# A ninth weight slot in an encoder layer's mixture of experts: the residual sums move into the rows buffer, and LayerNorm 2's constants are fetched last

## The chip, the cores and the metric

One core of a Trainium2 chip runs the whole program. The metric is the device time of one execution in microseconds; the times of before are three executions. Five engines work side by side and wait for each other by semaphores: PE (TensorE, matrix products), DVE (VectorE), ACT (ScalarE), POOL (GpSimd) and SP (SyncE, which here does nothing but issue transfers). The transfers run on 16 DMA engines.

## The reference, cut to what matters

One layer for 256 prompt frames and 32 sample frames of width 1024: LayerNorm 0, a combined projection, sparse attention and causal pooling, an output projection, LayerNorm 1, then a mixture of experts (top 4 of 32, softmax over the kept logits) and LayerNorm 2. What the change touches is the end:

```
h1 = LN1(2**0.25 * h + mix)                      # 288 rows of 1024
for e in range(32):
    gu   = h1 @ w1[e] + b1[e]                    # w1[e]: 1024 x 2048, f32, 8 MB
    gate = min(gu[:, :1024], 7); up = clip(gu[:, 1024:], -7, 7)
    act  = (up + 1) * gate * sigmoid(1.702 * gate)
    out += gates[:, e] * (act @ w2[e] + b2[e])   # w2[e]: 1024 x 1024, f32, 4 MB
y = LN2(2**0.25 * h1 + out)
```

All 32 experts' weights in f32, 32 x 12 MB (MB of 2^20 bytes here and for slots), are read once, and are nearly all that the program reads.

## The kernel before

**Passes.** Each expert's rows are handled in passes of 64 rows (BLK). With these inputs there are 32 passes, one for an expert, in a runtime loop over pairs: an even pass 2i and an odd pass 2i+1, and a last pair written out after the loop. In a pass (`expert` on PE, L981) the rows gathered before are multiplied by w1 (`up_products`, L891: eight parts k of 128 features; 64 products of L905), DVE and ACT make the clamped SwiGLU (L1629 to L1636, L1267), PE turns the result and multiplies by w2 (`down_products`, L921: two halves, 16 products of L931 each), and the product is added, weighted by the gates, to the sums of all 288 rows (`combine`, L965 on PE; `accumulate`, L1651 on DVE, for three tiles of 128 rows). While it does so it gathers the rows of the next pass (`gather_rows`, L869) from `rows_b`: the normalised rows split once, before the first pass, into three bf16 parts (ACT L1239 and L1242, DVE L1611 and L1614).

**Slots.** A pass needs 12 MB of weights. They come in eight slots of 2 MB (SLOT): `ring` slots 0 and 1 hold the first half of w1 of an even pass, `late` (two slots) that of an odd pass; ring slots 2 and 3 hold the second half of w1 (its third and fourth part) of every pass, and ring slots 4 and 5 the two halves of w2 of every pass. PE frees a slot when its last product has read it (`slot_free`, `odd_free`; slot 3's stands for the end of all up products). So before the loop eight slots are filled: pass 0's six and pass 1's first half.

**Order of the fetches.** SP issues them in an order written out by hand, each behind a wait for its slot; what stands behind a waiting issue waits too. For the first four pairs (WIDE_PAIR = 4, passes 0 to 7 releasing) it is `in_order_of_release` (L494), in narrow fetches of 2 MB: first half of pass 2i+2, rest (slots 2, 3, 4, 5) of 2i+1, first half of 2i+3, rest of 2i+2. Then LayerNorm 2's two constants are fetched (L514, L515; 512 KB each, spread over 128 partitions). Then comes `in_order_of_use` (L502) in wide fetches of 4 MB, each for a pair of slots and behind the release of both: slots 2 and 3 of 2i+1, slots 4 and 5, first half of 2i+2, slots 2 and 3, slots 4 and 5, first half of 2i+3. POOL counts up the second slot's semaphore for a wide fetch. The last pairs are narrow again.

**Buffers.** `rows` holds the layer's rows and, after the split into bf16 parts, nothing more: its tiles 1 and 2 take LayerNorm 2's constants (`ln2`), its tile 0 small things of the last pass. The sums live in `out_acc`, 12 KB per partition of `area`, a buffer that the input projection's and the output projection's weights had before; small scratch of the routing, the expert biases in bf16 (`bias_parts`) and the pooling's running sums are in `area` as well.

**The end.** After the last pass PE adds its two halves to the sums in PSUM (`start_sum`, `add_last`), DVE takes the statistics (L1698), centres with the constants (L1706), ACT and POOL or DVE finish, and three transfers write the result.

Of the kernel before, what the change touches and what calls it, by code (L numbers as in the profile page):

```python
# [22 lines left out]
P = 128  # L23
# [16 lines left out]
def encoder_kernel(nc, ins, outs):  # L40
# [32 lines left out]
    with ExitStack() as ctx:  # L73
# [7 lines left out]
        ring = sb("ring", [P, NSLOT, SLOT])  # L81

        area = sb("area", [P, KT * IN])
# [39 lines left out]
        out_acc = area[:, KT * D:KT * D + NT * D].rearrange("p (t n) -> p t n", t=NT)  # L123
        sums_a = area[:, KT * D:KT * D + 4 * UW].rearrange("p (g n) -> p g n", g=4)
        sums_b = area[:, KT * D + 4 * UW:KT * D + 8 * UW].rearrange("p (g n) -> p g n", g=4)
        BP = KT * D + NT * D

        bias_parts = area[0:3 * NE, BP:BP + 3 * F // 2].bitcast(BF16)
        last_u = area[0:POOL_PAST, BP + 3 * F // 2:BP + 3 * F // 2 + D].rearrange("p (s c) -> p s c", s=2)
        assert BP + 3 * F // 2 + D <= KT * IN  # L130
        flat = area[:, BP + 3 * F // 2:BP + 3 * F // 2 + D]
# [25 lines left out]
        spare = ring[:, 2:6, :].rearrange("p s n -> p (s n)")  # L157
# [21 lines left out]
        probs = carve(spare, 8 * 288)  # L179
        assert used[0] <= 4 * SLOT  # L180
# [4 lines left out]
        pick = carve(area, NT * BLK).bitcast(BF16).rearrange("p (t h s) -> p t h s", t=NT, h=2)  # L185
        g_sb = carve(area, F // 2)
# [10 lines left out]
        last_giveT = rows[:, 0, 0:TOKP]  # L197
        last_y = rows[:, 0, TOKP:TOKP + D // 2]
        ln2 = rows[:, 1:3, :]
# [34 lines left out]
        odd_free = [sem(f"odd_free{s}") for s in range(2)]  # L234
        bias_in = sem("bias_in")
# [119 lines left out]
        w1_t = ring[:, 0:4, :].rearrange("p s (k n) -> p (s k) n", k=2)  # L355
        w1_odd = late[:, :].rearrange("p (k n) -> p k n", k=4)
        w2_t = ring[:, 4:6, :].rearrange("p s (c n) -> p s c n", c=4)
# [42 lines left out]
        def _(sp):  # L400
# [31 lines left out]
            for s in range(2):  # L432
                sp.dma_start(ring[:, s, :], w1_part(0, s)).then_inc(w_in_slot[s], 16)
# [15 lines left out]
            sp.dma_start(ring[:, 2, :], w1_part(0, 2)).then_inc(w_in_slot[2], 16)  # L449
            sp.wait_ge(lastu_sb, 1)  # L450
            sp.dma_start(pool_prompt[0, 0], last_u[:, 0, :]).then_inc(rows_out, 16)
            sp.dma_start(pool_sample[0, 0], last_u[:, 1, :]).then_inc(rows_out, 16)
# [3 lines left out]
            sp.dma_start(ring[:, 3, :], w1_part(0, 3)).then_inc(w_in_slot[3], 16)  # L456
# [3 lines left out]
            for h in range(2):  # L460
                sp.dma_start(ring[:, 4 + h, :], w2_v[0, h]).then_inc(w_in_slot[4 + h], 16)
# [5 lines left out]
            def first_half(i, e, odd, wide):  # L467

                base, ready, free = (late[:, :], w_in_odd, odd_free) if odd else \
                    (ring[:, 0:2, :].rearrange("p s n -> p (s n)"), w_in_slot, slot_free)  # L470
# [10 lines left out]
            def rest(p, e, wide):  # L481

                for s in (2, 4) if wide else (2, 3, 4, 5):
                    if wide:
                        src = w1_v[col(e), 1] if s == 2 else w2_whole[col(e)]
                        dst = ring[:, s:s + 2, :]
                        sp.wait_ge(slot_free[s + 1], p)
                    else:
                        src = w1_part(col(e), s) if s < 4 else w2_v[col(e), s - 4]
                        dst = ring[:, s, :]  # L490
                    sp.wait_ge(slot_free[s], p)
                    sp.dma_start(dst, src.rearrange("e p n -> p (e n)")).then_inc(w_in_slot[s], 16)

            def in_order_of_release(i):  # L494

                even = expert_of(sp, 2 * i + 2)
# [5 lines left out]
            def in_order_of_use(i, wide):  # L502

                rest(2 * i + 1, expert_of(sp, 2 * i + 1), wide)
                even = expert_of(sp, 2 * i + 2)
                first_half(i, even, False, wide)
                rest(2 * i + 2, even, wide)
# [13 lines left out]
            sp.dma_start(y_prompt[0, P:2 * P, :], out_acc[:, 1, :]).then_inc(final_out, 16)  # L521
# [3 lines left out]
        def _(pool):  # L525
# [50 lines left out]
            pool.wait_ge(ln_in[2], 32)  # L576
            with pool.Fori(WIDE_PAIR, last_wide(pool)) as i:
                for first, p in ((w_in_slot, 2 * i + 1), (w_in_odd, 2 * i + 2)):
                    for s in (2, 4):
                        pool.wait_ge(w_in_slot[s], 16 * (p + 1))  # L580
                        pool.sem_inc(w_in_slot[s + 1], 16)
# [4 lines left out]
            nc.gpsimd.tensor_tensor(out_acc[:, 0, :], out_acc[:, 0, :], ln2[:, 1, :], ALU.add).then_inc(result[0], 1)  # L586
# [3 lines left out]
        def _(pe):  # L590
# [300 lines left out]
            def up_products(x, e, i, odd):  # L891
# [5 lines left out]
                for k in range(KT):  # L897
                    if k % 2 == 0 and k < 4:
                        pe.wait_ge((w_in_odd if odd else w_in_slot)[k // 2], 16 * (i + 1))
                    elif k % 2 == 0:  # L900
                        pe.wait_ge(w_in_slot[k // 2], 16 * (e + 1))
                    w = w1_odd[:, k] if odd and k < 4 else w1_t[:, k]
# [4 lines left out]
                    if k % 2 == 1 and k < KT - 1:  # L907
                        last.then_inc((odd_free if odd and k < 4 else slot_free)[k // 2], 1)
# [4 lines left out]
                last.then_inc(slot_free[3], 1)  # L913
# [124 lines left out]
            def start_sum(t, e):  # L1038
# [4 lines left out]
                for g in range(2):  # L1043
                    mm(ps_sum[t][0:n, g, :], ident[0:n, 0:n], out_acc[0:n, t, g * 512:(g + 1) * 512],
# [14 lines left out]
        def _(act):  # L1059
# [151 lines left out]
            copy(last_u[:, :, :], ps[0:POOL_PAST, 4:6, :]).then_inc(lastu_sb, 1)  # L1211
# [28 lines left out]
            for t in range(NT):  # L1240
                act.wait_ge(part_rest, t + 1)
                copy(rows_b[:, t, 1, :], rows[:, t, :]).then_inc(part_mid, 1)  # L1242
# [48 lines left out]
            nc.scalar.activation(out_acc[:, 0, :], out_acc[:, 0, :], ACT.Copy, scale=rstd[:, 0:1]).then_inc(scaled, 1)  # L1291
# [3 lines left out]
            nc.scalar.activation(ps_sum[1], out_acc[:, 1, :].rearrange("p (g n) -> p g n", g=2), ACT.Copy,  # L1295
# [4 lines left out]
            act.dma_start(y_prompt[0, 0:P, :], out_acc[:, 0, :]).then_inc(final_out, 16)  # L1300
            act.wait_ge(result[2], 1)
            act.dma_start(y_sample[0], out_acc[0:TS, 2, :]).then_inc(final_out, 16)
# [4 lines left out]
        def _(dve):  # L1307
# [293 lines left out]
            for t, (_, n, _) in enumerate(tiles):  # L1601
# [3 lines left out]
            v.tensor_scalar(giveT[:, :], out_acc[:, 0, 0:TOKP], 0.0, None, ALU.mult).then_inc(giveT_ready, 1)  # L1605
            v.tensor_scalar(y_sb[:, :], out_acc[:, 0, :], 0.0, None, ALU.mult).then_inc(y_ready, 1)

            dve.wait_ge(x_gathered, 1)
            for t in range(NT):
                dve.wait_ge(part_high, t + 1)  # L1610
                v.tensor_tensor(rows[:, t, :], rows[:, t, :], rows_b[:, t, 0, :], ALU.subtract).then_inc(part_rest, 1)  # L1611
            for t in range(NT):
                dve.wait_ge(part_mid, t + 1)
                v.tensor_tensor(rows_b[:, t, 2, :], rows[:, t, :], rows_b[:, t, 1, :], ALU.subtract).then_inc(split_ready, 1)  # L1614
# [23 lines left out]
            def swiglu_half(q, e):  # L1638

                g_q, u_q = quads(g_sb, q), quads(u_sb, q)  # L1640
                dve.wait_ge(slot_free[3], e + 1)
# [9 lines left out]
            def accumulate(t, comb, want, done, src=ps_c):  # L1651
                _, n, _ = tiles[t]
                dve.wait_ge(comb, want)
                acc = out_acc[0:n, t, :].rearrange("p (h n) -> p h n", h=2)
# [4 lines left out]
            def expert(e, last=False):  # L1659
# [15 lines left out]
                swiglu(slot_free[3], gate_ready, sig_ready, up_ready, prod_ready, e + 1, h_ready)  # L1675
# [27 lines left out]
            def centre(t):  # L1703

                n = tiles[t][1]
                v.scalar_tensor_tensor(halves(out_acc[0:n, t, :]), ps_sum[t][0:n], moments[0:n, t, 0:1],  # L1706
# [10 lines left out]
            v.tensor_tensor(halves(out_acc[:, 1, :]), ps_sum[1], halves(ln2[:, 1, :]), ALU.add).then_inc(result[1], 1)  # L1717
            centre(2)
            row = out_acc[0:TS, 2, :]
# [29 lines left out]
```

## Time and profile before

| | us |
|---|---|
| three executions | 1094.59, 1095.67, 1095.62 |
| their median | 1095.62 |
| the profiled execution | 1094.63 |
| its span, first to last instruction | 1092.8 |

The granted TensorE clock is 0.997 over the span. Busy in the span: PE 1039.7 us, DVE 399.3, ACT 238.2, POOL 15.1. Matmul ends are modelled, so a busy PE is not PE at its peak. "us to landing" of a transfer is counted from its issue on SP to the semaphore that says it has arrived, and so holds its time in the queue. Numbers at the start of a row are us from the span's start.

### The profile page before, as it was taken

The page shows a single profiled execution, that of the slowest core. Times are in us where ns is not written, and L with a number is a line of the kernel's source. Part 1 is how long each engine was busy: PE and PEld are TensorE (multiplying, and loading weights), DVE is VectorE, ACT ScalarE, POOL GpSimd, SP SyncE. Part 2 cuts the span into 40 slices and gives each one's busy share as a digit, 9 for nine tenths or more (in the row PEclk, how much of TensorE's full clock was granted, in tenths as well). Part 3 has the DMA queues.
Part 4 walks back from the last instruction along what each step waited for, and adds up shares of the span by engine and source line. Part 5 has one row for each costly group of instructions (what it writes and reads, how often), then busy time and mean ns, then how long its engine had stood idle before and what let it go on. Part 6 is the DMA issues. An engine that isn't in the chain of part 4 may idle for free.

```text
span 1092.8 us, 13939 instructions
## 1 busy us (share of the span) xinstructions
PE 1039.7 (95%) x5251; PEld 424.5 (39%) x5252; DVE 399.3 (37%) x721; ACT 238.2 (22%) x472; POOL 15.1 (1%) x28
## 2 busy tenths in 40 slices
PE   8989999999999999999999999999999999999996
PEld 7755463333333333333333333333333333333332
DVE  7894275333332233333222233333332322323226
ACT  3334123112222112222211122222211111222112
POOL 1003000000000000000000000000000000000000
PEclk9999999999999999999999999999999999999999
DMA  9750538999999999999999999999999999999991
GB/s 318 293 231 3 231 154 361 426 428 430 427 428 431 428 432 431 428 435 428 435 428 435 429 434 429 434 429 434 429 434 429 434 429 434 431 433 422 427 428 76
DMA packets 28556, 421.81 MB, mean 386 GB/s; under 512 B 5325, under 2 KB 5965, under 8 KB 11546
## 3 DMA queue, kind: packets, MB, share of 16 engines
q1 hardware_dynamic: 28346, 420.93, 91.1%
q10 hardware_dynamic: 192, 0.66, 0.2%
q8 instruction: 10, 0.16, 0.1%
q14 instruction: 8, 0.07, 0.0%
HBM read 420.11 MB, written 1.46 MB: 386 GB/s over the span
## 4 chain that ended last, share of the span: by engine, by line
PE 54%; DMA 34%; DVE 10%; issue 1%; ACT 0%; SPq 0%; DVEq 0%; ACTq 0%
DMA ring<-in_w_dram 34%; PE ps L905 30%; PE ps L931 10%; PE ps L751 3%; PE ps L633 3%; PE ps L968 2%; DVE area L1655 2%; DVE late L1420 1%; PE ps L884 1%; DVE area L1633 1%; DVE area L1636 1%; DVE area L1629 1%; DVE late L1419 1%; DVE area L1630 1%; PE ps L612 1%
## 5 line engine op out<-in xcount | busy, mean ns | idle before, releaser
L905 PE MATMUL ps<-ring,area 128*64 128x512 f32 x1536 | 341.0, 594 | 16.2 <-DMA ring<-in_w_dram 16.2
L931 PE MATMUL ps<-ring,area 128*64 128x512 f32 x992 | 224.9, 595 | 0.0
L905 PEld LDWEIGHTS ps<-ring,area 128*64 128x64 f32 x1536 | 107.3, 137 | 226.0 <-issue 189.9
L1655 DVE TENSOR_TENSOR area<-area,ps 128x1024 f32<-128x1024 f32 (+1 forms) x96 | 116.5, 1214 | 55.5 <-PE ps L968 55.5
L1629 DVE TENSOR_SCALAR area<-ps 128x512 f32<-128x512 f32 x31 | 21.4, 691 | 272.3 <-PE ps L905 272.3
L905 PE MATMUL ps<-late,area 128*64 128x512 f32 x512 | 116.1, 595 | 0.0
L931 PEld LDWEIGHTS ps<-ring,area 128*64 128x64 f32 x992 | 67.5, 136 | 120.7 <-issue 118.3
L1267 ACT ACTIVATE area<-area 128x512 f32<-128x512 f32 x31 | 19.5, 630 | 404.5 <-DVE area L1629 404.5
L1621 DVE SCALAR_TENSOR_TENSOR y_sb<-ps,gcol,y_sb 64x512 fp32r<-64x512 f32 x62 | 46.5, 750 | 98.4 <-ACT y_sb L1228 98.0
L968 PE MATMUL ps<-y_sb,giveT 128*128 128x512 f32 x192 | 69.5, 444 | 11.8 <-DVE area L1655 11.8
L875 PE MATMUL ps<-area 128*64 128x512 bf16 x558 | 66.1, 382 | 0.0
L1228 ACT ACTIVATE y_sb<-ps,gcol 64x512 fp32r<-64x512 f32 x62 | 42.3, 683 | 92.5 <-PE ps L931 91.7
L633 PE MATMUL ps<-late,area 128*128 128x288 f32 (+1 forms) x224 | 58.5, 418 | 0.0
L905 PEld LDWEIGHTS ps<-late,area 128*64 128x64 f32 x512 | 35.2, 136 | 58.4 <-issue 54.9
L1547 DVE TENSOR_TENSOR area<-iota_slot,kv_rows 128x384 bf16 (+2 forms) x33 | 18.0, 546 | 105.3 <-issue 105.2
L1275 ACT COPY area<-ps 128x512 f32<-128x512 f32 x31 | 18.1, 585 | 154.3 <-PE ps L884 154.3
L633 PEld LDWEIGHTS ps<-late,area 128*128 128x128 f32 (+1 forms) x224 | 41.9, 191 | 14.4 <-issue 2.2
L968 PEld LDWEIGHTS ps<-y_sb,giveT 128*128 128x128 f32 x192 | 29.1, 191 | 44.6 <-issue 26.8
L875 PEld LDWEIGHTS ps<-area 128*64 128x64 bf16 x558 | 29.0, 109 | 33.6 <-issue 11.3
L1267 ACT ACT_TABLE_LOAD x31 | 39.8, 1283 | 0.5
L1553 DVE CAST sel<-same_exp 96x64 bf16 (+1 forms) x32 | 6.1, 191 | 82.7 <-PE ps L931 82.7
L751 PE MATMUL ps<-area,late 128*128 128x512 f32 (+1 forms) x96 | 35.2, 595 | 0.6 <-DVE late L1484 0.6
(239 smaller groups left out, 654.9 us busy)
## 6 DMA issues: line engine op xcount, KB each, us to landing
ring<-in_w_dram SPq DMA_DIRECT2D x50, 4096.0 KB, 21.7
ring<-in_w_dram SPq DMA_DIRECT2D x60, 2048.0 KB, 16.5
late<-in_w_dram SPq DMA_DIRECT2D x10, 4096.0 KB, 26.7
late<-in_w_dram SPq DMA_DIRECT2D x12, 2048.0 KB, 15.2
area<-in_w_o_dram SPq DMA_DIRECT2D x1, 4096.0 KB, 13.8
area<-in_w_in_dram SPq DMA_DIRECT2D x1, 2560.0 KB, 16.5
area<-in_w_in_dram SPq DMA_DIRECT2D x1, 2336.0 KB, 9.4
area<-in_w_in_dram SPq DMA_DIRECT2D x1, 2048.0 KB, 20.5
```

Source lines behind the costliest of these rows:

```text
L633: last = mm(ps[0:w, proj_bank(i), 0:TOK], w_in_sb[chunk][:, j, c0:c0 + w], tokT[:, j, :], start=(j == 0), stop=(j == KT - 1))
L751: last = mm(dst, mixed[:, k, t0:t0 + n], w_o_sb[:, k, half * 512:(half + 1) * 512], start=(start and k == ks[0]), stop=(stop and k == ks[-1]))
L875: last = mm(ps[g * BLK:(g + 1) * BLK, 2, :], one[:, t, 0, :], rows_b[:, t, part, g * 512:(g + 1) * 512], start=(t == 0 and part == 0), sto ...
L905: last = mm(ps_gu[g * BLK:(g + 1) * BLK, c, :], x[:, spot(k), :], half_of(w, c, g), start=False, stop=(k == KT - 1))
L931: last = mm(ps_y[g * BLK:(g + 1) * BLK, :], hT[:, c, h, :], w2_t[:, h, c, g * 512:(g + 1) * 512], start=False, stop=(h == 1 and c == 3))
L968: last = mm(dst[:, g, :], giveT[:, t * P:(t + 1) * P], y_sb[:, g * 512:(g + 1) * 512], start=True, stop=True)
L1228: nc.scalar.activation(y_sb[0:BLK, g * 512:(g + 1) * 512], ps_y[r, :], ACT.Copy, scale=gcol[r, :]).then_inc(done, 1)
L1267: nc.scalar.activation(sig_sb, g_sb, ACT.Sigmoid, scale=SWIGLU_ALPHA).then_inc(sig_ready, 1)
L1275: copy(xT, ps_x).then_inc(xT_ready, 1)
L1621: ins = v.scalar_tensor_tensor(y_sb[BLK:P, g * 512:(g + 1) * 512], ps_y[r, :], gcol[r, :], y_sb[0:BLK, g * 512:(g + 1) * 512].bitcast(F32) ...
L1629: v.tensor_scalar(g_sb, ps_gu[:, 0, :], LIMIT, None, ALU.min).then_inc(gate, 1)
L1655: v.tensor_tensor(acc, acc, src[0:n, :, :], ALU.add).then_inc(done, 1)
```

## The change

The sums are kept in `rows` itself: DVE splits the rows into the three bf16 parts by way of scratch in the first pass's own buffers (`rest_of`), then multiplies `rows` by the residual factor in place, and `accumulate`, `start_sum` and LayerNorm 2 work on `rows`. `ring`, `area` become views of one tensor `store`, laid so that the freed end of `area` (`extra`, 2 MB over the partitions) borders on ring slot 2. The ninth slot holds the third part of w1 of odd passes; their fourth part goes to ring slot 2, and the even passes keep slots 2 and 3. So slot 2 is used twice in a pair: by the even pass's third and by the odd pass's fourth part, and slot 3 once. `up_done` takes the place of slot 3's release. The third part of pass 1 is fetched before the loop, behind slot 3's fetch. The pair behind the first four becomes narrow, in order of use. LayerNorm 2's constants go to ring slot 0 and are issued after all weights. `last_giveT` and `last_y` go to ring slot 1, `last_u` beside the attention's scratch, copied by two instructions; `flat`, `bias_parts` and the pooling's sums change their place.

```diff
-        ring = sb("ring", [P, NSLOT, SLOT])
-        area = sb("area", [P, KT * IN])
+        store = sb("store", [P, NSLOT * SLOT + KT * IN])
+        area = store[:, 2 * SLOT:2 * SLOT + KT * IN]
+        REST = 2 * SLOT + KT * IN
+        def ring(s, n=1):
+            at = s * SLOT if s < 2 else REST + (s - 2) * SLOT
+            return store[:, at:at + n * SLOT]
+        extra = store[:, REST - SLOT:REST]
+        extra_pair = store[:, REST - SLOT:REST + SLOT]
...
+        rest_of = [area[:, GX + i * F:GX + (i + 1) * F] for i in (0, 1, 0)]
+        ln2 = ring(0)[:, 0:2 * D].rearrange("p (i n) -> p i n", i=2)
...
+            sp.wait_ge(pool_diff, 1)
+            sp.dma_start(extra, w1_part(1, 2)).then_inc(w_in_extra, 16)
...
+            def third_even(i, e):
+                sp.wait_ge(up_done, 2 * i + 2)
+                fetch(ring(2), w1_part(col(e), 2), w_in_slot[2])
+            def fourth_even(i, e):
+                sp.wait_ge(up_done, 2 * i + 1)
+                fetch(ring(3), w1_part(col(e), 3), w_in_slot[3])
+            def third_odd(i, e):
+                sp.wait_ge(extra_free, i)
+                fetch(extra, w1_part(col(e), 2), w_in_extra)
+            def fourth_odd(i, e):
+                sp.wait_ge(slot_free[2], i + 1)
+                fetch(ring(2), w1_part(col(e), 3), w_in_slot[2])
+            def down(p, e, wide):
+                sp.wait_ge(slot_free[4], p)
+                if wide:
+                    sp.wait_ge(slot_free[5], p)
+                    fetch(ring(4, 2), w2_whole[col(e)], w_in_slot[4])
+                    return
+                fetch(ring(4), w2_v[col(e), 0], w_in_slot[4])
+                sp.wait_ge(slot_free[5], p)
+                fetch(ring(5), w2_v[col(e), 1], w_in_slot[5])
             def in_order_of_release(i):
...
                 first_half(i, even, False, False)
-                rest(2 * i + 1, expert_of(sp, 2 * i + 1), False)
-                first_half(i, expert_of(sp, 2 * i + 3), True, False)
-                rest(2 * i + 2, even, False)
+                fourth_odd(i, odd)
+                fourth_even(i, even)
+                down(2 * i + 1, odd, False)
+                first_half(i, next_odd, True, False)
+                third_odd(i + 1, next_odd)
+                third_even(i, even)
+                down(2 * i + 2, even, False)
+            def odd_rest(i, wide, third=True):
+                odd = expert_of(sp, 2 * i + 1)
+                if wide:
+                    sp.wait_ge(slot_free[2], i + 1)
+                    sp.wait_ge(extra_free, i)
+                    fetch(extra_pair, w1_v[col(odd), 1], w_in_extra)
+                else:
+                    if third:
+                        third_odd(i, odd)
+                    fourth_odd(i, odd)
+                down(2 * i + 1, odd, wide)
+            def in_order_of_use(i, wide, third=True):
+                odd_rest(i, wide, third)
                 even = expert_of(sp, 2 * i + 2)
                 first_half(i, even, False, wide)
+                if wide:
+                    sp.wait_ge(up_done, 2 * i + 2)
+                    fetch(ring(2, 2), w1_v[col(even), 1], w_in_slot[2])
+                else:
+                    third_even(i, even)
+                    fourth_even(i, even)
+                down(2 * i + 2, even, wide)
                 first_half(i, expert_of(sp, 2 * i + 3), True, wide)
...
             with sp.Fori(0, WIDE_PAIR) as i:
                 in_order_of_release(i)
-            sp.wait_ge(split_ready, NT)
+            in_order_of_use(WIDE_PAIR, False, third=False)
+            with sp.Fori(WIDE_PAIR + 1, end_wide) as i:
+                in_order_of_use(i, True)
+            in_order_of_use(end_wide, False)
+            odd_rest(end_wide + 1, False)
+            sp.wait_ge(slot_free[0], end_wide + 2)
             sp.dma_start(ln2[:, 0, :], ln2_g[0].partition_broadcast(P)).then_inc(ln_in[2], 16)
             sp.dma_start(ln2[:, 1, :], ln2_b[0].partition_broadcast(P)).then_inc(ln_in[2], 16)
-            with sp.Fori(WIDE_PAIR, end_wide) as i:
-                in_order_of_use(i, True)
-            in_order_of_use(end_wide, False)
-            rest(2 * end_wide + 3, expert_of(sp, 2 * end_wide + 3), False)
...
-            for t, (_, n, _) in enumerate(tiles):
-                v.tensor_scalar(out_acc[0:n, t, :], rows[0:n, t, :], RESIDUAL, None, ALU.mult).then_inc(acc_init, 1)
-            dve.wait_ge(acc_init, NT)
...
+            dve.wait_ge(x_gathered, 1)
+            take_high(0)
+            take_high(1)
+            take_mid(0)
+            dve.wait_ge(split_ready, 1)
+            take_high(2)
+            take_mid(1)
+            dve.wait_ge(part_rest, 3)
+            for t, (_, n, _) in enumerate(tiles):
+                v.tensor_scalar(rows[0:n, t, :], rows[0:n, t, :], RESIDUAL, None, ALU.mult).then_inc(acc_init, 1)
+            take_mid(2)
```

`take_high(t)` is the subtraction of L1611 written to `rest_of[t]` behind ACT's first part; `take_mid(t)` is L1614, from `rest_of[t]`.

## Rows read from the trace of the kernel before

**Rows 1.** The page: PE's busy time, and GB/s in 40 equal slices.

```profile
PE 1039.7 (95%) x5251; PEld 424.5 (39%) x5252; DVE 399.3 (37%) x721; ACT 238.2 (22%) x472; POOL 15.1 (1%) x28
GB/s 318 293 231 3 231 154 361 426 428 430 427 428 431 428 432 431 428 435 428 435 428 435 429 434 429 434 429 434 429 434 429 434 429 434 431 433 422 427 428 76
```

**Rows 2.** The chain that ended last: start us, us, what (passes 8, 11, 13, 14).

```profile
386.50 3.44 PE ps L905 x16
390.27 10.47 PE ps L905 x48
405.85 3.44 PE ps L931 x16
...
470.39 3.44 PE ps L905 x16
...
534.48 7.11 PE ps L905 x32
...
563.61 7.11 PE ps L905 x32
```

**Rows 3.** The waits: who waited for whom: us in total, times, longest.

```profile
PE ps L905 <- DMA ring<-in_w_dram: 16.2, 17, 1.0
```

**Rows 4.** Windows ahead of the loop: busy of the engines, PEclk, DMA share, GB/s.

```profile
140.00:145.00 5.00, 5.00 (x28) 1.81 (x24) 2.69 (x5) 0.00 (x0) 0.00 (x0) 1.00 0.00 0
```

**Rows 5.** L492, five single issues (start), each with us to landing under it.

```profile
L492 SPq DMA_DIRECT2D ring<-in_w_dram x1: 333/333/333, 205.2 to 205.2; - x1
DMA to landing us min/median/max: 14.4/14.4/14.4
...
L492 SPq DMA_DIRECT2D ring<-in_w_dram x1: 333/333/333, 372.9 to 372.9; - x1
DMA to landing us min/median/max: 22.9/22.9/22.9
...
L492 SPq DMA_DIRECT2D ring<-in_w_dram x1: 333/333/333, 386.2 to 386.2; - x1
DMA to landing us min/median/max: 19.4/19.4/19.4
...
L492 SPq DMA_DIRECT2D ring<-in_w_dram x1: 343/343/343, 414.2 to 414.2; - x1
DMA to landing us min/median/max: 13.4/13.4/13.4
...
L492 SPq DMA_DIRECT2D ring<-in_w_dram x1: 332/332/332, 470.1 to 470.1; - x1
DMA to landing us min/median/max: 15.7/15.7/15.7
```

**Rows 6.** L446 and L461, issued on an empty queue, us to landing under each.

```profile
L446 SPq DMA_DIRECT2D area<-in_w_o_dram x1: 402/402/402, 61.5 to 61.5; - x1
DMA to landing us min/median/max: 13.8/13.8/13.8
...
L461 SPq DMA_DIRECT2D ring<-in_w_dram x2: 362/391/420, 122.8 to 123.2; - x2
DMA to landing us min/median/max: 7.2/10.1/12.9
```

**Rows 7.** LayerNorm 2's second constant: its issue, and its us to landing (last).

```profile
387.17 0.43 SPq L515 DMA_DIRECT2D rows<-in_ln_b_dram  x1
...
rows<-in_ln_b_dram SPq DMA_DIRECT2D x1, 512.0 KB, 21.0
```

**Rows 8.** DVE's timeline in the first pass: start, us, what [idle before, releaser].

```profile
172.96 0.56 DVE L1547 TENSOR_TENSOR area<-iota_slot,kv_rows 128x384 bf16 x1 [0.47 <-issue]
177.10 0.69 DVE L1629 TENSOR_SCALAR area<-ps 128x512 f32<-128x512 f32 x1 [3.58 <-PE ps L905]
```

**Rows 9.** The end of the chain: the last weight fetch, and the first statistics.

```profile
1048.12 21.72 DMA ring<-in_w_dram
...
1079.15 1.31 DVE stats L1698 x2
```

More of the change, by code:

```diff
@@ L179, in encoder_kernel @@
         probs = carve(spare, 8 * 288)
+        last_u = carve(spare, 4 * P)
         assert used[0] <= 4 * SLOT
@@ L354, in encoder_kernel @@
         w2_whole = w2[0].rearrange("e (p q) n -> e p (q n)", q=KT)
-        w1_t = ring[:, 0:4, :].rearrange("p s (k n) -> p (s k) n", k=2)
-        w1_odd = late[:, :].rearrange("p (k n) -> p k n", k=4)
-        w2_t = ring[:, 4:6, :].rearrange("p s (c n) -> p s c n", c=4)
+        w1_halves = [[at.rearrange("p (k n) -> p k n", k=4) for at in two]
+                     for two in ((ring(0, 2), ring(2, 2)), (late[:, :], extra_pair))]
+        w2_t = ring(4, 2).rearrange("p (s c n) -> p s c n", s=2, c=4)
         x_views = [x_prompt[0].rearrange("(t p) d -> p t d", p=P), x_sample[0]]
@@ L479, in first_half, with fetch @@
                         .then_inc(ready[s], 16)
[L481 to L492, printed above, removed]
+            def fetch(dst, src, ready):
+                sp.dma_start(dst, src.rearrange("e p n -> p (e n)")).then_inc(ready, 16)
@@ L494, in in_order_of_release @@
+            def down(p, e, wide):
[7 more added lines that the diff above has]
+                fetch(ring(5), w2_v[col(e), 1], w_in_slot[5])
             def in_order_of_release(i):
-                even = expert_of(sp, 2 * i + 2)
+                even, odd, next_odd = (expert_of(sp, 2 * i + q) for q in (2, 1, 3))
@@ L573, in _ @@
             nc.gpsimd.tensor_copy(bias_parts, bias_f).then_inc(bias_ready, 1)
[L576 to L581, printed above, removed]
+            with pool.Fori(WIDE_PAIR + 1, last_wide(pool)) as i:
+                for second, half, first, count, p in (
+                        (w_in_extra, w_in_slot[2], w_in_slot, 16 * (i + 1), 2 * i + 1),
+                        (w_in_slot[2], w_in_slot[3], w_in_odd, 16 * (2 * i + 3), 2 * i + 2)):
+                    pool.wait_ge(second, count)
+                    pool.sem_inc(half, 16)
+                    pool.wait_ge(w_in_slot[4], 16 * (p + 1))
+                    pool.sem_inc(w_in_slot[5], 16)
                     pool.wait_ge(first[0], 16 * (i + 2))
@@ L897, in up_products @@
                 for k in range(KT):
-                    if k % 2 == 0 and k < 4:
+                    if k in (0, 2):
                         pe.wait_ge((w_in_odd if odd else w_in_slot)[k // 2], 16 * (i + 1))
-                    elif k % 2 == 0:
-                        pe.wait_ge(w_in_slot[k // 2], 16 * (e + 1))
-                    w = w1_odd[:, k] if odd and k < 4 else w1_t[:, k]
+                    elif k == 4 and odd:
+                        pe.wait_ge(w_in_extra, 16 * (i + 1))
+                    elif k == 6 and not odd:
+                        pe.wait_ge(w_in_slot[3], 16 * (i + 1))
+                    elif k in (4, 6):
+                        pe.wait_ge(w_in_slot[2], 16 * (e + 1))
+                    w = w1_halves[odd][k // 4][:, k % 4]
                     for c in range(2):
@@ L906, in up_products @@
                                       start=False, stop=(k == KT - 1))
-                    if k % 2 == 1 and k < KT - 1:
-                        last.then_inc((odd_free if odd and k < 4 else slot_free)[k // 2], 1)
+                    if k in (1, 3):
+                        last.then_inc((odd_free if odd else slot_free)[k // 2], 1)
+                    elif k == 5:
+                        last.then_inc(extra_free if odd else slot_free[2], 1)
                     if k == 1:
@@ L1716, in _ @@
             dve.wait_ge(scaled, 2)
-            v.tensor_tensor(halves(out_acc[:, 1, :]), ps_sum[1], halves(ln2[:, 1, :]), ALU.add).then_inc(result[1], 1)
+            v.tensor_tensor(halves(rows[:, 1, :]), ps_sum[1], halves(ln2[:, 1, :]), ALU.add).then_inc(result[1], 1)
             centre(2)
-            row = out_acc[0:TS, 2, :]
+            row = rows[0:TS, 2, :]
             dve.wait_ge(centred, 3)
```

89 lines of the change are left out of this document (44 added, 45 removed).

## Prediction

> **What bounds the kernel now.** First the slices of the page: almost no transfer in the fourth and the sixth slice, then an unbroken 422 to 435 GB/s until the last, while PE is 95% busy [rows 1]. Both look full, so the chain decides. Up to 500 us it holds no DMA: a pass follows a pass every 27.96 us (from 386.50 to 470.39 are three), PE and a few DVE steps. From 534 us on, each pass's second half of the up products starts when a ring fetch lands, every 29.13 us [rows 2]. So there are two stages. In the first the weights are ahead of PE; in the second 12 MB per pass is the bound. PE waits there for DMA only 16.2 us in all [rows 3]: that is all that an earlier stream could ever give.
>
> The stream of narrow fetches: the one issued at 205.2 lands 14.4 us later, at 219.6; the one at 386.2 lands at 405.6; 38 lie from the first to the last, so one every 4.895 us. Wide ones (4 MB) come every 29.13/3 = 9.71 us. The second half of the weights for down of pass 11 (both halves in one fetch, I call it w2(11)) is issued at 470.1, when pass 10 ends, and lands at 485.8; that of pass 9 is issued at 414.2 and lands at 427.6 [rows 5]. Between the two landings are six wide fetches in 58.2 us, 9.70 each: no gap. From 485.8 to the last landing at 1048.12 + 21.72 = 1069.8 [rows 9] are 52 wide and 16 narrow fetches, 52 x 9.71 + 16 x 4.895 = 583.2 us against 584.0: no gap either. **So the end is the landing of w2(11) plus a constant**, and I ask when it lands after the change.
>
> **The change, part by part.** *The extra fetch before the loop.* 2 MB, issued by SP right after slot 3's, as pool_diff comes before the pool products that SP has already waited for. DMA moves nothing in the row of 140 to 145 us [rows 4], and the two fetches of down weights behind it are wanted only after pass 0's up products, whose end DVE sees at 177.10 [rows 8]: price nothing; without that cover 4.9 us. *Its worth:* 4.9 us less to stream later.
>
> *LayerNorm 2's constants* leave the middle: the second lands 21.0 us after 387.17, at 408.2, 2.6 us behind slot 5's 405.6 [rows 5, 7]. At the end they sit behind the last weights: 1069.8 + 2.6 = 1072.4, and DVE wants them at 1079.15 [rows 9]: hidden by 6.7 us. SP's wait ahead of them, for slot 0, is over with the first quarter of the last but one pass, and no other fetch stands behind them.
>
> *One more narrow pair:* six wide fetches become twelve: 12 x 4.895 - 6 x 9.71 = 0.5 us.
>
> *An unbroken stream* would put 11 narrow and 2 wide fetches between 405.6 and w2(11): 405.6 + 53.8 + 19.4 = 478.9 in place of 485.8, **6.9 us earlier**. But SP's waits don't allow it, and this is the step on which I forecast.
>
> *A new stall in pass 8.* Ring slot 2 now serves odd passes' fourth part and even passes' third. For an even pass it is free only when the up products before have ended, where the fourth part's fetch stood in the old order: in pass 7 that is the fetch issued at 372.9, landing at 395.8 [rows 5]. Before, that was the fourth part; now it is the third, wanted two eighths of the up products sooner: 390.27 + 10.47/3 = 393.8 [rows 2]. PE waits 2.0 us. In pass 2 the same place lands at 219.6 and is wanted at 390.27 + 3.5 - 6 x 27.96 = 226.0, so no wait; every two passes the margin shrinks by 12 x 4.895 - 55.92 = 2.8 us: 6.4, 3.6, 0.8, then -2.0. Everything behind it in pass 8 (products, slot releases, the passes to come) is 2.0 us late; PE itself would wait in the DMA-bound stage anyway, but SP's issues are tied to it.
>
> *Two gaps in the stream.* After slot 5 (405.6) the fourth part of pass 9 lands at 410.5. Next in SP's order stands w2(9), freed by the first half of pass 8's down products: 405.85 + 3.44 + 0.1 + 2.0 = 411.4 [rows 2]. The queue is empty by then (the constants filled it before, and a wide fetch issued earlier). Two 2 MB fetches issued on an empty queue at 122.8 took 12.9 us from the second's issue 0.4 us later, 13.3 in all [rows 6], 3.5 over their stream time: they land at 424.7, 4.4 us late. Eight narrow and one wide later, 473.6, w2(11) is due; SP may issue it at 470.1 + 2.0 = 472.1. What does an issue 1.5 us ahead of an empty queue cost? Below: nothing, landing 473.6 + 9.7 = 483.3, since 3.6 ahead cost nothing at 414.2 (427.6 is 2 x 9.7 behind 408.2). Above: all of a lone 4 MB, 13.8 us [rows 6], landing 485.9. I take 13.4, by the two fetches of 16 KB rows that are nearest in kind, **485.5: 0.3 us earlier than before**, bounds 2.5 earlier to 0.1 later. The first gap then hardly counts: a smaller one only lets the queue run empty before 472.1.
>
> The Trainium skill (DMA: Bandwidth & Descriptors, section "Anatomy of one DMA") gives a transfer some 2.0 us fixed plus its bytes at 436 GB/s. By that 4 MB would be an estimated 11.6 us and w2(11) would land at 483.7, 2.1 us earlier; the row of 13.8 us here does not agree, so the sum goes by the row.
>
> *The rest.* Behind w2(11) order and sizes are as before; w2(12) is issued at 472.1 + 27.96 = 500.1, 4.8 us ahead of the landing before it (485.5 + 2 x 9.71), so no third gap. DVE's split of the rows goes back and forth with ScalarE, with the same ten large operations as before: I let it end up to 1 us later than the 172.5 that the one-hot's start at 172.96 shows; the first SwiGLU waits for PE until 177.10 [rows 8], a cover of 3.6 us, beyond which each us counts in full. last_u in two copies, and POOL's relays counting other semaphores: nothing, behind the pool products and half a pass.
>
> **Sum.** The profiled execution took 1094.63; -0.3 gives 1094.3. The median shown is 1.0 above that execution, so I predict 1095.3.
>
> **The rivals.** *A: the stream stays unbroken* (the queue at 410 is longer than I count, or SP's order hides the issue): 1095.6 - 6.9 = 1088.7. For it: PE has 16.2 us of DMA wait to give. Against: w2(11) can't be issued before pass 10 ends, so it needs PE ahead of where the rows have it.
>
> *B: the restart is cheap, or pass 8 doesn't stall.* w2(11) at 483.3 to 483.8: 2.0 to 2.5 us, 1093.4; the page's rule above belongs here. For it: the fetch is issued before the queue is empty. Against: the 13.3 and 13.8 us.
>
> *C: slower.* Until w2(11) is issued each us that PE loses is a us of the end. Pass 8's stall hangs on where the stream stands after 46 narrow fetches (6 from each of seven passes and 4), 225 us: 1% of rate is 2.2 us of stall. The ring's slots move to other addresses; were they 1.5% slower, w2(11) would land 3.3 us later than forecast: 1098.6; it decides from 0.9% on. Against: the 38 fetches, whose mean I use, already went into two tensors at different addresses. If the slot were not filled ahead at all (D), w2(11) would land behind a stream 4.9 us longer, at 488.2: 1098.0; against that speak the idle 15 us.
>
> **Chances.** About 0.2%, 2.2 us, is what can be told from no change. Forecast 0.54, all within; B 0.21, 0.10 of it just beyond 2.2 us; A 0.12, faster; C and D 0.13, slower. Faster 0.22, same 0.65, slower 0.13. The range leaves out the full A and the far end of C: 1090.5 to 1098.3.
>
> **What would show it.** A first wait of PE at the third part in pass 8, about 2 us; DMA below 430 GB/s at about 411 and 473 us and full around them; w2(11) landing near 485.5; LayerNorm 2's statistics starting as soon as the sums are there. I am wrong if w2(11) lands before 483, if DVE waits at the end, or if the first pass starts late.

## The result: 0.13% slower, and the profile after

| | before | after |
|---|---|---|
| median of 22 runs each, us | 1095.54 (1094.59 to 1096.38) | 1096.57 (1094.44 to 1100.19) |
| ratio after/before | | 1.0013 [1.0007, 1.0019] |
| profiled execution, us | 1094.63 | 1096.59 |
| its span, us | 1092.8 | 1094.7 |
| granted TensorE clock over the span | 0.997 | 0.994 |
| landing of the last weights, us | 1069.8 | 1071.8 |

The medians differ by 1.0 us, the profiled executions by 2.0. Below, these two are laid side by side; after's is at its median, before's 0.9 under its own. The landing of the last weights, 2.0 us later, accounts for the whole difference between the two.

The page of after, PE's busy time and the GB/s in 40 equal slices:

```profile
PE 1041.0 (95%) x5251; PEld 424.8 (39%) x5252; DVE 399.3 (36%) x721; ACT 238.5 (22%) x473; POOL 15.2 (1%) x28
GB/s 320 289 231 3 307 154 360 428 427 429 429 427 429 429 398 342 430 412 433 430 437 425 438 424 438 424 439 424 438 430 432 432 431 438 424 438 422 426 427 118
```

Against [rows 1] the fifth slice has risen from 231 to 307: the extra 2 MB was fetched ahead of the loop. But the 15th, 16th and 18th slice (383 to 438 and 465 to 493 us) have fallen to 398, 342 and 412, where before had 432, 431 and 435. Against 430 GB/s these three slices lack 2.0, 5.6 and 1.1 us of stream, 8.7 together. That is more than the 6.9 us that the prediction put down for an unbroken stream, so the holes gave back the 4.9 us of the extra 2 MB and the rest, and 1.8 more.

The chain that ended last (start us, us, what), cut to the passes' first products around the hole, two passes behind it, the last weights and the statistics:

```profile
358.70 3.44 PE ps L971 x16
...
373.09 23.48 DMA store<-in_w_dram
...
396.61 8.51 PE ps L971 x32
...
418.84 3.44 PE ps L971 x16
...
446.80 3.44 PE ps L971 x16
...
474.76 3.44 PE ps L971 x16
...
1049.99 21.82 DMA store<-in_w_dram
...
1081.12 1.30 DVE stats L1779 x2
```

In [rows 2] no DMA stands in the chain here. Now a fetch holds pass 8 until 396.57, and pass 11 begins at 474.76 where it began at 470.39. From 474.76 on, order and pace are those of before.

PE's timeline of the second half of pass 8's up products (in brackets the idle time before it and who ended it):

```profile
396.61 8.48 PE L971 MATMUL ps<-store 128*64 128x512 f32 x32 [2.60 <-DMA store<-in_w_dram]
```

and the 2-us windows around it (busy us of PE, PEld, DVE, ACT, POOL, each with its count; then PEclk, DMA share, GB/s), with those of the first hole in the stream and one of the second:

```profile
394.00:396.00 2.00, 0.01 (x2) 0.00 (x0) 0.00 (x0) 0.00 (x0) 0.00 (x0) 1.00 0.96 410
396.00:398.00 2.00, 1.39 (x4) 0.53 (x6) 0.00 (x0) 0.00 (x0) 0.00 (x0) 0.51 1.02 434
398.00:400.00 2.00, 2.00 (x8) 0.61 (x6) 0.00 (x0) 0.00 (x0) 0.00 (x0) 0.63 1.00 426
400.00:402.00 2.00, 2.00 (x12) 0.64 (x10) 0.00 (x0) 0.00 (x0) 0.00 (x0) 1.00 1.02 434
...
408.00:410.00 2.00, 1.59 (x8) 1.02 (x10) 1.18 (x2) 1.03 (x2) 0.00 (x0) 1.00 0.39 164
410.00:412.00 2.00, 2.00 (x12) 0.70 (x10) 1.14 (x1) 0.00 (x0) 0.00 (x0) 1.00 0.02 8
412.00:414.00 2.00, 2.00 (x11) 0.70 (x8) 0.19 (x1) 0.00 (x0) 0.00 (x0) 1.00 0.00 0
414.00:416.00 2.00, 2.00 (x11) 0.85 (x12) 1.16 (x1) 1.17 (x4) 0.00 (x0) 1.00 0.62 139
...
476.00:478.00 2.00, 2.00 (x12) 0.46 (x8) 0.64 (x1) 1.10 (x1) 0.00 (x0) 1.00 0.70 279
```

**Where the time went.** Pass 8 lasts from 386.66 to 418.84, 32.18 us for 27.96: 4.2 us more. 2.60 are the wait for the third part. After that idle time the granted clock is 0.51 and 0.63, against 1.00 on both sides: PE is at the lower level, 1.2 GHz, nearly all of the first window and much of the second. The 32 products of the second half take 8.5 us; two thirds of the 10.47 in [rows 2] are 7.0. That is 1.5 us more, and the two make 4.1 of the 4.2. After this PE is 4.4 us behind before (446.80 against 442.43), since pass 8 began 0.16 later.

SP's issues of the three fetches that matter (start; under each its us to landing): the third part in pass 8, w2(9)'s first half, w2(11):

```profile
L497 SPq DMA_DIRECT2D store<-in_w_dram x1: 332/332/332, 373.1 to 373.1; - x1
DMA to landing us min/median/max: 23.5/23.5/23.5
...
L497 SPq DMA_DIRECT2D store<-in_w_dram x1: 333/333/333, 413.8 to 413.8; - x1
DMA to landing us min/median/max: 7.3/7.3/7.3
...
L497 SPq DMA_DIRECT2D store<-in_w_dram x1: 333/333/333, 474.5 to 474.5; - x1
DMA to landing us min/median/max: 13.2/13.2/13.2
```

w2(11) is issued 4.4 us later than in [rows 5] and takes 13.2 in place of 15.7, since it is issued only 2.6 us ahead of the landing in front of it (477.1) and has less of a queue to wait for: 487.7 against 485.8. Those 1.9 us are the 2.0 at the end.

### The profile page after: what moved, and what is told of

The parts are those of the page before. It is cut to its first block, busy times and chain, and to the rows that moved or that the text cites. A ratio compares the mean times of both kernels' runs of the same rounds, so it can differ in the third digit from the quotient of the medians.

```text
span 1094.7 us, 13935 instructions
## 1 busy us (share of the span) xinstructions
PE 1041.0 (95%) x5251; PEld 424.8 (39%) x5252; DVE 399.3 (36%) x721; ACT 238.5 (22%) x473; POOL 15.2 (1%) x28
## 4 chain that ended last, share of the span: by engine, by line
PE 53%; DMA 35%; DVE 10%; issue 1%; ACT 0%; SPq 0%; DVEq 0%; ACTq 0%
DMA store<-in_w_dram 34%; PE ps L971 28%; PE ps L999 10%; PE ps L813 3%; PE ps L695 3%; PE ps L1036 2%; DVE rows L1736 2%; PE ps L946 1%; DVE late L1489 1%; DVE store L1714 1%; DVE store L1717 1%; DVE store L1710 1%; DVE late L1488 1%; DVE store L1711 1%; PE ps L674 1%
## 5 line engine op out<-in xcount | busy, mean ns | idle before, releaser
L971 PE MATMUL ps<-store 128*64 128x512 f32 x1536 | 342.5, 596 | 16.8 <-DMA store<-in_w_dram 16.7
L999 PE MATMUL ps<-store 128*64 128x512 f32 x992 | 224.9, 595 | 0.0
L971 PEld LDWEIGHTS ps<-store 128*64 128x64 f32 x1536 | 107.6, 137 | 227.7 <-issue 191.0
L1736 DVE TENSOR_TENSOR rows<-rows,ps 128x1024 f32<-128x1024 f32 (+1 forms) x96 | 116.5, 1215 | 55.5 <-PE ps L1036 55.5
L971 PE MATMUL ps<-late,store 128*64 128x512 f32 x512 | 116.1, 595 | 0.0
L999 PEld LDWEIGHTS ps<-store 128*64 128x64 f32 x992 | 67.5, 136 | 120.7 <-issue 118.3
L937 PE MATMUL ps<-store 128*64 128x512 bf16 x558 | 66.1, 382 | 0.0
L695 PE MATMUL ps<-late,store 128*128 128x288 f32 (+1 forms) x224 | 58.6, 418 | 0.0
L971 PEld LDWEIGHTS ps<-late,store 128*64 128x64 f32 x512 | 35.3, 136 | 58.4 <-issue 54.9
L695 PEld LDWEIGHTS ps<-late,store 128*128 128x128 f32 (+1 forms) x224 | 42.0, 192 | 14.3 <-issue 2.1
L937 PEld LDWEIGHTS ps<-store 128*64 128x64 bf16 x558 | 28.9, 109 | 33.6 <-issue 11.4
L813 PE MATMUL ps<-store,late 128*128 128x512 f32 (+1 forms) x96 | 35.2, 595 | 0.6 <-DVE late L1553 0.6
```

The costliest lines, as they stand in the source:

```text
L695: last = mm(ps[0:w, proj_bank(i), 0:TOK], w_in_sb[chunk][:, j, c0:c0 + w], tokT[:, j, :], start=(j == 0), stop=(j == KT - 1))
L813: last = mm(dst, mixed[:, k, t0:t0 + n], w_o_sb[:, k, half * 512:(half + 1) * 512], start=(start and k == ks[0]), stop=(stop and k == ks[-1]))
L937: last = mm(ps[g * BLK:(g + 1) * BLK, 2, :], one[:, t, 0, :], rows_b[:, t, part, g * 512:(g + 1) * 512], start=(t == 0 and part == 0), sto ...
L971: last = mm(ps_gu[g * BLK:(g + 1) * BLK, c, :], x[:, spot(k), :], half_of(w, c, g), start=False, stop=(k == KT - 1))
L999: last = mm(ps_y[g * BLK:(g + 1) * BLK, :], hT[:, c, h, :], w2_t[:, h, c, g * 512:(g + 1) * 512], start=False, stop=(h == 1 and c == 3))
L1736: v.tensor_tensor(acc, acc, src[0:n, :, :], ALU.add).then_inc(done, 1)
```

## The experiments

The theory: *the end is w2(11)'s landing, and w2(11) cannot be issued before pass 10 ends; the extra slot's 4.9 us are lost because its fetch, as placed, stalls pass 8, and because the queue runs empty before SP may issue w2(9) and w2(11).* The rivals: the new addresses make the stream slower; the constants, now last, hold the end; the switch to 4 MB fetches one pair later costs it. Each ratio is against runs of the kernel before on the same chip. "From pass 0" is the last weights' landing less the start of pass 0's up products in the profiled execution: that start scatters by up to 4 us (161.72 to 165.88) between profiled executions and would blur the readings. It is 907.3 for before and 909.2 for after. It has a scatter of its own: in single executions one landing comes 0.3 to 1.5 us late though the queue is not empty.

| kernel | median us | ratio, 95% | from pass 0, us |
|---|---|---|---|
| third_first | 1092.84 | 0.998 [0.997, 0.999] | 904.6 |
| unbroken_order | 1089.08 | 0.9947 [0.9934, 0.9961] | 902.3 |
| busy_wait | 1095.65 | 1.0001 [0.9989, 1.0012] | 908.2 |
| three_pairs | 1095.59 | 1.0004 [0.9995, 1.0013] | 907.3 |
| late_constants_only | 1095.17 | 0.999 [0.9979, 1.0] | 907.2 |
| before_pe_late | 1097.52 | 1.0019 [1.001, 1.0028] | 909.3 |
| third_first_pe_late | 1095.99 | 1.0001 [0.9992, 1.001] | 907.6 |

**third_first.** After, but in the last pair in order of release the even pass's third part is issued three fetches sooner, ahead of the next odd pass's first half and third part:

```diff
+            def in_order_early(i):
...
+                down(2 * i + 1, odd, False)
+                third_even(i, even)
+                first_half(i, next_odd, True, False)
+                third_odd(i + 1, next_odd)
+                down(2 * i + 2, even, False)
...
-            with sp.Fori(0, WIDE_PAIR) as i:
+            with sp.Fori(0, WIDE_PAIR - 1) as i:
                 in_order_of_release(i)
+            in_order_early(WIDE_PAIR - 1)
```

> In the fourth pair (passes 6 and 7 releasing) the third part of pass 8 is fetched ahead of pass 9's first three quarters; nothing else differs from the changed kernel. Theory: the end is the landing of the wide fetch of pass 11's down weights, w2(11), plus a constant, and that fetch is issued when pass 10 ends, so the 4.1 us that PE loses in pass 8 (2.6 waiting, the rest at a lower granted clock) are lost at the end too. Then: no wait of PE for a fetch in pass 8, granted clock 1.00 there, pass 9 starts at about 414.6 in place of 418.8, w2(11) is issued at 470.3 and lands at about 483.7, and the time is some 4 us under the changed kernel's, about 1092.8 (0.9975 of before). Rival 1 (PE waits for DMA later anyway, so an earlier wait is only moved): as the changed kernel, 1.001. Rival 2 (the new addresses slow the stream in the DMA-bound stage): the wait goes, the time hardly moves.

Measured: 1092.84. The chain has pass 8's products in one piece, and w2(11) is issued 3.7 us sooner than in after and lands at 483.0:

```profile
387.18 3.44 PE ps L984 x16
...
390.95 10.47 PE ps L984 x48
...
415.14 3.44 PE ps L984 x16
```

```profile
L497 SPq DMA_DIRECT2D store<-in_w_dram x1: 332/332/332, 470.8 to 470.8; - x1
DMA to landing us min/median/max: 12.1/12.1/12.1
```

The only thing removed is the stall, 4.2 us of pass 8; the median is 3.7 lower. So the stall is what made the change slower. Where one fetch stands in the order, with the same slots and the same bytes, decides its sign.

**unbroken_order.** As third_first, with the sooner third part in the fourth and the fifth pair and the 4 MB fetches only from the eighth pair on, so that down weights fetched half by half leave no hole:

```diff
-    WIDE_PAIR = 4
+    WIDE_PAIR = 6
...
+            with sp.Fori(0, 3) as i:
                 in_order_of_release(i)
-            in_order_of_use(WIDE_PAIR, False, third=False)
+            in_order_early(3)
+            in_order_early(4)
+            in_order_of_use(5, False, third=False)
+            in_order_of_use(6, False)
```

> The ninth slot and the late constants are kept; only SP's order differs: three pairs in order of release, two more like the fourth pair of third_first (third part of the next even pass ahead of the next odd pass's first three quarters), then two narrow pairs in order of use, and wide fetches only from the eighth pair on. Theory: no fetch is then issued on a queue that is about to run empty, so the stream is unbroken from the first release on: 2 MB (4.9 us) and the constants (2.6 us) less, three narrow pairs in place of wide ones 1.4 us more: 6.1 us under before, about 1089.4 (0.9944), DMA share near 1.0 in all windows from 170 us to the last landing, no clock drop before the DMA-bound stage. Rival (the ninth slot's layout or the place of the constants costs something by itself): DMA unbroken and yet not under 0.998.

Measured: 1089.08, the fastest of all, 6.4 us under before on the same chip (1095.50) and near the forecast's rival A (1088.7). Its page:

```profile
GB/s 320 294 233 3 309 155 361 424 429 428 427 429 428 421 431 427 430 425 429 429 427 440 428 437 428 429 439 427 430 435 429 438 426 432 437 427 424 429 427 103
```

From the eighth slice to the last but one none is below 421. The addresses are the new ones, the constants come last, and the slot's 4.9 us are there: slower addresses and late constants are out as causes.

**busy_wait.** After, with nine small products on `ident` (18 matrix instructions in the trace) in the middle of pass 8's up products, so that PE works through the wait:

```diff
                 for k in range(KT):
+                    if k == 4:
+                        keep_warm(fill, bank=3)
...
+            expert(8, 4, False, fill=9)
```

> The changed kernel with its stall in pass 8, but PE fills it: in that pass alone nine small products into a spare bank stand ahead of the wait for the third part (about 2.6 us, the length of the wait). Theory: the second half of pass 8's up products took 8.5 us in place of 7.1 because the granted clock fell to its lower level after the wait; kept busy, PE is granted 1.00 there, the half takes 7.1 us, w2(11) is issued at about 473.0 in place of 474.5 and the end is some 1.4 us earlier than the changed kernel's (about 1095.2, 0.9997 of before). Rival: the 1.4 us are a second wait inside (the fourth part's semaphore): 8.5 us and the time as they were.

Measured: 1095.65, whose range overlaps after's, so the time alone doesn't decide. The chain and a window of pass 8 do:

```profile
393.49 3.58 PE ps L973 x16
...
397.07 2.21 PE ps L674 x18
...
399.28 7.06 PE ps L973 x32
```

```profile
400.00:402.00 2.00, 2.00 (x12) 0.72 (x10) 0.00 (x0) 0.00 (x0) 0.00 (x0) 1.00 1.00 426
```

With PE busy while the fetch comes, the granted clock stays 1.00 and the second half takes 7.06 us for 8.51; pass 8 is 30.34 us long for 32.18. So the clock's part of the stall, 1.45 us, is shown to come from the idle time. The other 0.4 us is the fetch, which here leaves PE a gap of 2.1 us (397.07 to 399.2) where it was 2.60:

```profile
L497 SPq DMA_DIRECT2D store<-in_w_dram x1: 333/333/333, 376.2 to 376.2; - x1
DMA to landing us min/median/max: 23.0/23.0/23.0
```

w2(11) is issued 2.1 us sooner than in after, counted from pass 0, but takes 14.6 us to land for 13.2, so the end is only 1.0 us sooner; why this fetch took longer stays open.

**three_pairs.** After, with the 4 MB fetches one pair sooner, as many narrow fetches as before:

```diff
-    WIDE_PAIR = 4
+    WIDE_PAIR = 3
```

> The changed kernel with WIDE_PAIR 3 in place of 4: the order of release ends a pair earlier. Theory: the third part of pass 8 is then early and PE does not wait, but the first wide fetch of down weights is now pass 9's, issued when pass 8 ends (414.2) on a queue that is about to run empty, so it lands at about 427.5 as before the change (427.6), and everything behind is as before: 1095.4 (1.000). Rival (only the stall of pass 8 cost anything): as third_first, 0.9975 or better. The other rival (addresses): as the changed kernel, 1.001 or more.

Measured: 1095.59, the time of before. Pass 8 takes its weights in order and does not stall, but w2(9), now one fetch, cannot be issued before 415.1, 2.6 us ahead of the landing in front of it, and lands at 428.0; in [rows 5] it lands at 427.6. The stream had run dry once before, ahead of the first half of w2(7), as it did in after ahead of that of w2(9). Against 430 GB/s the windows from 350 to 358 us (90, 16, 98 and 311) lack 5.6 us, those from 414 to 418 (131 and 279) 2.1: together what the slot and the constants save, 4.9 and 2.6. Two of these windows, then w2(9):

```profile
352.00:354.00 2.00, 2.00 (x12) 0.49 (x8) 0.00 (x0) 0.00 (x0) 0.00 (x0) 1.00 0.04 16
...
414.00:416.00 2.00, 2.00 (x14) 0.66 (x10) 0.29 (x1) 0.98 (x2) 0.00 (x0) 1.00 0.31 131
...
L497 SPq DMA_DIRECT2D store<-in_w_dram x1: 333/333/333, 415.1 to 415.1; - x1
DMA to landing us min/median/max: 12.9/12.9/12.9
```

The slot is filled ahead, pass 8 doesn't stall, and nothing is won: the stream runs dry at the points that are tied to PE.

**late_constants_only.** Before, with LayerNorm 2's constants behind all weights and nothing else changed but POOL's wait for them, which moves along:

```diff
             with sp.Fori(0, WIDE_PAIR) as i:
                 in_order_of_release(i)
-            sp.wait_ge(split_ready, NT)
-            sp.dma_start(ln2[:, 0, :], ...
...
             rest(2 * end_wide + 3, expert_of(sp, 2 * end_wide + 3), False)
+            sp.wait_ge(split_ready, NT)
+            sp.dma_start(ln2[:, 0, :], ...
```

> The kernel before with one part of the change: LayerNorm 2's constants fetched after all weights, still into the rows buffer; eight slots and SP's order as before. Theory: without the constants the wide third and fourth part of pass 9 land at 415.3 in place of 417.8, but the wide fetch of pass 9's down weights can't be issued before pass 8 ends (414.2), 1.1 us ahead of an empty queue, and lands some 13.2 us later, 427.4 in place of 427.6: the time is within 0.3 us of before (0.9998), and the 1 MB taken out of the middle is worth nothing there. Rival (1 MB less in a stream that bounds the kernel is 2.6 us less): 0.9976.

Measured: 0.999 [0.9979, 1.0], a median 0.3 us lower; the rival's 2.6 us (0.9976) lie just outside the interval. The 2.6 us of transfer leave the stream, but while the landing of the fetch before w2(9) moves from 417.9 to 416.4, w2(9)'s moves only from 427.6 to 427.4 (counted from pass 0, 2.1 us and 0.8 us sooner), as its issue at 414.8 is now only 1.6 us ahead of the landing in front of it:

```profile
L492 SPq DMA_DIRECT2D ring<-in_w_dram x1: 333/333/333, 414.8 to 414.8; - x1
DMA to landing us min/median/max: 12.6/12.6/12.6
```

**before_pe_late.** Before, with the nine products in pass 8: PE about 2 us late, stream unchanged (the same two edits as busy_wait).

> The kernel before, with nine small products into a spare bank ahead of the third part of the up products in pass 8 alone: PE is busy 2.2 us longer there, at full clock. Theory: in the kernel before the stream is full at that place (pass 11's down weights are issued 6 us ahead of the landing before them), so PE's loss there is taken back by its later waits for DMA: time within 0.4 us of before (1.000 to 1.0004). Rival (PE's pace up to 500 us is on the path, as the chain of waits has it): 2.2 us more, 1.002.

Measured: 1.0019 [1.001, 1.0028], 2.0 us slower: a miss. I had looked at w2(11) alone, which in before is issued 6.0 us ahead of the landing in front of it. The thin place is w2(9). In before it is issued 3.7 us ahead. Here it is 2.1 (the fetch in front, then w2(9)):

```profile
L492 SPq DMA_DIRECT2D ring<-in_w_dram x1: 343/343/343, 404.1 to 404.1; - x1
DMA to landing us min/median/max: 15.4/15.4/15.4
...
L492 SPq DMA_DIRECT2D ring<-in_w_dram x1: 343/343/343, 417.3 to 417.3; - x1
DMA to landing us min/median/max: 12.2/12.2/12.2
```

and by then the stream has run dry (the windows' last number is GB/s):

```profile
416.00:418.00 2.00, 2.00 (x14) 0.80 (x12) 0.03 (x1) 0.72 (x2) 0.00 (x0) 1.00 0.34 139
418.00:420.00 2.00, 2.00 (x12) 0.58 (x10) 1.47 (x2) 1.93 (x2) 0.00 (x0) 1.00 0.92 262
```

Against 430 GB/s these two windows lack 2 x (1 - 139/430) + 2 x (1 - 262/430) = 2.1 us of stream, where the four windows around the same place in before, at 410, 377, 492 and 344, lack 0.5 and w2(9) lands 9.7 us behind the fetch in front of it, the pace of a full stream. So PE's loss reaches the end in the kernel before as well: its "DMA-bound" end already hung on PE by the issue of w2(9).

**third_first_pe_late.** third_first with the same nine products.

> third_first with the same nine products in pass 8. Theory: here the stream runs empty when pass 10 ends, so the same 2.2 us of PE move the issue of pass 11's down weights and with it the end by 2.2 us: about 1095.0 (third_first measured 1092.84), 0.9998 of before. Rival (the late third part itself, not PE's place, cost the changed kernel its time): as third_first, 0.998.

Measured: 1095.99, 3.1 us above third_first (3.0 from pass 0) for 2.2 us of products. w2(11) is issued 310.3 us after pass 0's start for 307.5 in third_first.

Without a stall, the same loss of PE time takes the gain away again. That PE's lost time reaches the end in full is shown by the two runs together (2.0 and 3.0 us for 2.2). Of the 0.8 above 2.2 here, 0.4 stood before pass 8, where PE waited for a fetch in pass 6; the rest stays open.

**The eight traces together.** In the four kernels where w2(9) is one fetch issued close to the landing in front (before, late_constants_only, before_pe_late, three_pairs), the last weights land 655.6, 655.6, 655.4 and 655.5 us after the issue of w2(9), though before_pe_late issues it 2.3 us later from pass 0. In after, third_first and third_first_pe_late they land 597.3, 597.1 and 597.3 us after the issue of w2(11), over a range of 4.4 us of that issue; busy_wait, with its slower fetch, has 598.4. So the end hangs on the *issue* of one fetch, and that on PE.

## Why the prediction was right and wrong

**Wrong: "A new stall in pass 8", by its size.** The place, the fetch and the cause were as forecast, the price was not: 2.0 us forecast, 4.2 measured. The missing term is the clock: I priced idle time of PE as idle time alone and let the products behind it run at full rate, but at the lower level they cost another 1.5. The sum had no room for that: its forecast was a gain of 0.3, the difference of a restart and a stall. With the 1.5 alone put in, it is an estimated 1.2 slower; the medians differ by 1.0.

The wait itself was 2.60, because the third part landed at 396.6 for 395.8 and was wanted 0.2 later. Rival C had named that a small lateness of the stream sets the stall. All 0.8 us of it came early, at one landing: the fetch issued at 194.4 in before and at 194.3 in after.

```profile
L478 SPq DMA_DIRECT2D late<-in_w_dram x1: 333/333/333, 194.4 to 194.4; - x1
DMA to landing us min/median/max: 10.5/10.5/10.5
...
L492 SPq DMA_DIRECT2D late<-in_w_dram x1: 333/333/333, 194.3 to 194.3; - x1
DMA to landing us min/median/max: 11.4/11.4/11.4
```

From there to the third part both streams need 190.9 us. In busy_wait the landing is not late, and PE's gap is 2.1 us, the 2.0 forecast. before_pe_late, with the slots of before, has such a landing too, 1.1 us late at 201.7. So this part belongs to the execution and not to the change; why such a landing is late stays open.

**"Two gaps in the stream": right in place.** The queue ran empty from 409 to 414, and the stream dipped at 474 to 480, to 279 GB/s at the lowest. A smaller dip that I had not forecast lies between them, at 434 to 440 (369, 344 and 352 GB/s); it hardly counts, as w2(11) waits for pass 10 all the same. w2(9)'s first half was issued at 413.8 for 411.4, w2(11) at 474.5 for 472.1: both 2.4 late, 2.2 from the stall and 0.2 from the start of pass 8. One step was wrong: I let both halves of w2(9) go at 411.4, but the second half's slot is free only when pass 8 ends, and it was issued at 418.6. That it landed at 426.9, just those 2.2 behind the forecast 424.7, is luck. For the restart of w2(11) I took 13.4 us and it was 13.2. In the other runs a 4 MB issue 1.6 to 2.6 us ahead of the landing in front took 12.1 to 12.9, but w2(11) in busy_wait 14.6: above the 13.8 of [rows 6] that I had as the upper bound. By the Trainium skill (DMA: Bandwidth & Descriptors, section "Anatomy of one DMA") I had estimated 11.6. The section gives its rule for transfers issued by GpSimd; these are issued by SyncE, and all measured values lie above it.

**"The end is the landing of w2(11) plus a constant": right.** 487.7 against 485.8 there, 1071.8 against 1069.8 at the end. With the forecast 485.5 and the measured 2.2 more of stall, less 0.2 of restart, plus 0.2 of start, the sum would have been 487.7, and the time of the profiled execution 1096.5; it was 1096.59. What I did not see is that in before w2(9) bounds the end as well (before_pe_late).

**"An unbroken stream" and rival A: right as a size, and rightly refused for this order.** 6.9 us forecast, 6.4 measured in unbroken_order, by another order of issue. Rival B's time (1093.4) is near what third_first gave, in which pass 8 doesn't stall.

**The costs put at nothing** held. The constants:

```profile
1050.85 0.42 SPq L579 DMA_DIRECT2D store<-in_ln_b_dram  x1
...
DMA to landing us min/median/max: 23.4/23.4/23.4
```

They land at 1074.3 and the statistics begin at 1081.12: 6.8 us hidden, forecast 6.7. DVE's split, in the timeline of the first pass:

```profile
171.44 1.21 DVE L1681 TENSOR_TENSOR store<-store 128x1024 bf16<-128x1024 f32 x1
175.50 0.56 DVE L1616 TENSOR_TENSOR store<-iota_slot,kv_rows 128x384 bf16 x1 [2.85 <-issue]
177.02 0.69 DVE L1710 TENSOR_SCALAR store<-ps 128x512 f32<-128x512 f32 x1 [0.96 <-PE ps L971]
```

The split ends at 172.65 for some 172.5 before, inside the 1 us that I allowed. But the one-hot behind it starts at 175.50 for 172.96 in [rows 8], after 2.85 us for which the profile shows no releaser; what they are stays open. The first SwiGLU still waits for PE, 0.96 in place of 3.58: it cost nothing, but the cover was thinner than I had counted.

One reading of [rows 1] was loose and changes nothing: the sixth slice moved 154 GB/s, which is not "almost no transfer".

## What to carry to other kernels

A buffer more, or bytes moved out of a stream that bounds the end, are worth their full price only if the order of issue never lets the queue run empty: find the fetch issued with the least lead before the landing in front of it, for here the end hung on that one and on whatever set its issue. When a slot comes free late in a pass, ask when the part that now lives in it is *wanted*, and place its fetch in the queue by that. Price a stall of TensorE with what the clock does to the products behind it.

## What the runs showed of the hardware

After 2.60 us of idle PE in pass 8, the granted clock was 0.51 and 0.63 in the two windows up to 400 us. PE's other 15 waits for DMA in these products, 14.1 us together, 1.0 at the longest and all behind 500 us, are part of a stage that shows the full clock:

```profile
500.00:1080.00 580.00, 553.93 (x2806) 202.34 (x2804) 170.07 (x223) 112.61 (x202) 0.00 (x0) 1.00 0.99 425
```

A 4 MB issue 3.7 us ahead of the landing in front of it (w2(9) in before) left at most 0.5 us of a hole in the stream; 2.1 us ahead (before_pe_late) it left 2.1. A landing is thus no sign that the queue is full until then: in after the last landing ahead of the first hole is at 411.2, but the windows from 408 and from 410 moved only 164 and 8 GB/s.

The times of after and of most kernels derived from it scatter more (1094.4 to 1100.2) than the first 22 of before (1094.6 to 1096.4), but later ones of before reach from 1093.7 to 1098.8. Part of it lies ahead of the loop and goes with the granted clock there. In busy_wait and third_first_pe_late, whose pass 0 starts last (165.9 and 165.8), it is 0.83 from 120 to 130 us and 0.79 from 150 to 158. In third_first and before_pe_late (163.3 and 163.4) it is 0.83 and 1.00, and in before, after and unbroken_order (161.7 to 162.6) 1.00 in both. What lowers it there stays open.
